# Streaming encoder step on one core: each half's first data loaded by the half ahead, semaphores cleared inside halves, another block order

## The reference: what is computed

```python
h = rms_norm(x, norm_g)
proj = h @ w_in        # 1024 -> 3912 columns, fifteen parts
# A: per query the 256 best keys by an indexer, softmax over these only
sc = relu(einsum('bthd,bsd->bths', iq, ik)); sc = einsum('bths,bth->bts', sc, iw)
sc = where(kpos // 64 <= qpos // 64, sc, -inf); idx = top_k(sc, 256)
ya = softmax(q . k[idx] / 8) @ v[idx] * silu(ag)      # 8 heads, 2 key heads
# B: gated linear recurrence (HGRN2), C: retention; each carries a 64x64 state per head
yb = rms_norm(gla(bq, 1 - f, bi, log f)) * silu(bg)
yc = rms_norm(retention(cq, ck, cv)) * silu(cg)
out = x + concat(ya, yb, yc) @ w_out
```

## Time and profile before

| | us |
|---|---|
| median of 3 runs (lowest, highest) | 3991.1 (3989.07, 3997.01) |
| the profiled execution's own time | 3998.49 |
| its span, first to last instruction | 3996.7 |
| TensorE busy | 3579.7 (90%) |
| VectorE busy | 2647.8 (66%) |
| ScalarE busy | 2324.3 (58%) |
| GpSimd busy | 1002.8 (25%) |
| mean granted clock of TensorE | 0.947 |

### The profile page before, as it was taken

One profiled execution on the slowest core, in us unless ns is written; L12 is line 12 of the kernel. 1 busy time (PEld: TensorE's weight loads), 2 busy tenths in 40 slices (PEclk: granted clock), 3 DMA queues, 4 the chain that ended last, 5 costly groups with the idle time before them and its releaser, 6 DMA issues. The chain is left out here.

```text
span 3996.7 us, 57114 instructions
## 1 busy us (share of the span) xinstructions
PE 3579.7 (90%) x17620; PEld 1677.0 (42%) x17620; DVE 2647.8 (66%) x6170; ACT 2324.3 (58%) x4386; POOL 1002.8 (25%) x1712
## 2 busy tenths in 40 slices
PE   6999999995789889898869999999768898899997
PEld 3555555551233333343335555555413333333433
DVE  7677777765766677565346666666666767776652
ACT  5333333335788888877323333333277888888762
POOL 0000000113543333334200000000145433333341
PEclk8999999996799999999989999999878999999998
DMA  5222222215201000011151111111152010000111
GB/s 187 86 79 80 79 80 79 78 55 137 79 24 35 31 24 21 22 38 36 39 201 37 38 39 39 42 38 34 36 131 78 18 39 23 23 25 20 39 39 39
DMA packets 175714, 226.60 MB, mean 57 GB/s; under 512 B 77632, under 2 KB 115520, under 8 KB 173696
## 3 DMA queue, kind: packets, MB, share of 16 engines
q1 hardware_dynamic: 175488, 224.06, 18.3%
HBM read 146.60 MB, written 77.38 MB: 56 GB/s over the span
## 5 line engine op out<-in xcount | busy, mean ns | idle before, releaser
L1524 ACT ACTIVATE signs<-sc,mid 128x1152 bf16<-128x1152 f32 (+14 forms) x720 | 974.9, 1355 | 278.4 <-POOL mid L1580 268.5
L426 PE MATMUL PJ<-w_in_hi,hTh 128*128 128x512 f16 (+2 forms) x2176 | 812.2, 373 | 18.4 <-DVE w_in_lo L937 16.7
L427 PE MATMUL PJ<-w_in_lo,hTh 128*128 128x512 f16 (+2 forms) x2176 | 810.8, 373 | 0.0
L429 PE MATMUL PJ<-w_in_hi,hTl 128*128 128x512 f16 (+3 forms) x1904 | 704.3, 370 | 0.0
L1429 PE MATMUL PV<-pt,va_p 128*65 128x512 f32 x1088 | 584.1, 625 | 73.3 <-ACT pt L1504 65.8
L1577 POOL TENSOR_SCALAR dlt<-cnta,stp 128x1 f32<-128x1 f32 (+1 forms) x720 | 293.0, 407 | 1075.9 <-ACT signs L1524 1072.5
L1672 DVE SCALAR_TENSOR_TENSOR sc<-rl,iwb,sc 128x512 f32<-128x512 f32 (+4 forms) x602 | 422.4, 718 | 208.3 <-ACT rl L1495 201.2
L1609 DVE CUSTOM_DVE_ANT_0 junkb<-AX,mneg 128x512 bf16<-128x512 f32 (+4 forms) x720 | 412.3, 601 | 74.1 <-PE AX L1374 55.0
L1580 POOL TENSOR_SCALAR mid<-mid,dlt,stp 128x1 f32<-128x1 f32 (+1 forms) x720 | 430.7, 598 | 75.6
L1495 ACT ACTIVATE rl<-AX 128x512 f32<-128x512 f32 (+5 forms) x688 | 347.1, 531 | 81.5 <-PE AX L1387 76.5
L1504 ACT ACTIVATE pt<-LG 128x512 f32<-128x512 f32 (+2 forms) x612 | 329.4, 553 | 92.8 <-PE LG L1414 88.4
(11 more groups left out here) (267 smaller groups left out, 5850.0 us busy)
## 6 DMA issues: line engine op xcount, KB each, us to landing
yt<-y_d SPq DMA_DIRECT2D x32, 512.0 KB, 3.5
out<-xr SPq DMA_DIRECT2D x32, 512.0 KB, 2.6
w_stage<-in SPq DMA_DIRECT2D x28, 512.0 KB, 4.1
w_d<-w_stage SPq DMA_DIRECT2D x56, 256.0 KB, 2.4
x<-in SPq DMA_DIRECT2D x16, 512.0 KB, 4.5
y_d<-ga SPq DMA_DIRECT2D x32, 256.0 KB, 2.0
q<-q_d SPq DMA_DIRECT2D x32, 256.0 KB, 2.9
stg<-in SPq DMA_DIRECT2D x32, 256.0 KB, 2.7
```

The costliest lines, as they stand in the source:

```text
L426: mm(out, hTh[:, par, c, 0:T], weights(g, c, wh), start=(c == 0), stop=False)
L427: mm(out, hTh[:, par, c, 0:T], weights(g, c, wl), start=False, stop=False)
L429: last = mm(out, hTl[:, par, c, 0:T], weights(g, c, wh), start=False, stop=(c == DC - 1))
L1524: A(signs[p][0:T, 0:W], sc[u % 3][0:T, 0:W], ACT.Sign, scale=-1.0, bias=small[u % 3]["mid"][0:T, :], accum_out=small[u % 3]["cnta"][0:T, : ...
```

## The change

*Buffers.* One tile `arena` as large as the 16 MB of weights, and x and the gains `ng`, now live through the whole kernel. The weights of a recurrent half fill the arena. In an attention half it holds the prompt's keys, queries, values, output weights, score buffers and others, laid out by hand (`in_arena`), so that the parts loaded first lie where the weights of groups that are used early lay. The row of ones is written once to device memory (`ones_d`) and loaded into the key tiles by DMA.

*Recurrence to attention.* While it is at block NB, SyncE loads for the attention half: the indexer's keys (4 DMAs), the first searched block's indexer queries and weights, the first q; behind the `kiT_c` wait the keys of both heads, the next indexer queries, two more q, the values. Only then do the stores of the keys of block NB follow. The states are stored a little earlier. The plan counts these loads as done.

*Attention to recurrence.* Ahead of the last store SyncE loads x of block 0, the gains and the weight groups 0 to 2 of the next layer (`next_layer`); the next half loads its constants and the groups 3 to 7.

*Semaphores.* Each half has its own set and GpSimd clears the other half's inside it; behind the last layer three engines share the rest.

*Order.* Another `seq`. *Retention.* Its transposes come behind the intra-chunk products, and `cqs` and `cqkT`'s copy accordingly.

The core of the diff:

```diff
+    BLOCKS = [1, 0, 3, 5, 7, 4, 6, 10, 12, 9, 11, 13, 14, 15, NB, 8, 2]
+    FIRST_SEARCHED = [b for b in BLOCKS if (b == NB and PAST + TS > K_S) or (b < NB and (b + 1) * P > K_P)][:2]
...
+    AHEAD = 3
...
+                if splits:
+                    load_x(0)
+                    sp.dma_start(ng[:], norm_g[l, :, :]).then_inc(gains, 16)
+                else:
+                    load_constants()
+                    for g in range(AHEAD, NG):
+                        load_group(go_own, g)
...
                     store_pairs(iq16_d, b, T, iqh, iql, st_iq)
+                    if b == NB:
+                        sp.wait_ge(proj, NG * NB + GI["cqk"] + 1)
+                        sp.wait_ge(st_ki, 64 * NB)
+                        load_prompt_keys(go_ahead, 2, 0)
+                        load_prompt_keys(go_ahead, 2, 1)
+                        sp.wait_ge(st_iq, 64 * NB)
+                        sp.wait_ge(st_v, 32 * NB)
+                        load_index_queries(go_ahead, 0, FIRST_SEARCHED[0])
+                        sp.wait_ge(proj, NG * NB + GI["iq"] + 1)
+                        sp.wait_ge(st_q, 64 * NB)
+                        load_queries(go_ahead, 0)
...
                     sp.wait_ge(kiT_c, b + 1)
+                    if b == NB:
+                        sp.wait_ge(proj, NG * NB + GI["kvi"] + 1)
+                        load_prompt_keys(go_ahead, 0, 0)
+                        load_prompt_keys(go_ahead, 1, 0)
+                        load_index_queries(go_ahead, 1, FIRST_SEARCHED[1])
+                        load_prompt_keys(go_ahead, 0, 1)
+                        load_prompt_keys(go_ahead, 1, 1)
+                        load_queries(go_ahead, 1)
+                        load_queries(go_ahead, 2)
+                        load_prompt_values(go_ahead, l)
+                        sp.wait_ge(sh_ok, 2 * NB + 1)
+                        for j in range(4):
+                            sp.dma_start(hg_s[l, j, :, :], head_square(S2, j)).then_inc(st_st, 16)
...
                     if b == 0 and prepares:
                         if splits:
                             sp.wait_ge(*low_done(len(chunks) - 1))
                         load_next(0)
+                    sp.wait_ge(yb_ok, 2 * b + 2)
...
                     project(t, T, par, "iq")
-                    pe.wait_ge(rpc_ok, t + 1)
-                    transposes(trv[1], [rpc[0:T, c * P:(c + 1) * P] for c in range(4)], T).then_inc(cqkT_ok, 1)
...
                     last.then_inc(atth_ok, 1)
+                    pe.wait_ge(rpc_ok, t + 1)
+                    transposes(trv[1], [rpc[0:T, c * P:(c + 1) * P] for c in range(4)], T).then_inc(cqkT_ok, 1)
                     project(t, T, par, "kvi")
...
                 rsqrt(x_ms, x_rs, rsx[:], ssx[:], 1)
+                for used in old:
+                    pool.sem_clear(used)
...
-            seq = [0, 1, 3, 8, 11, 9, 10, 12, 14, 13, 15, NB, 7, 6, 5, 4, 2]
+            seq = BLOCKS
...
+                    j0 = seq.index(0)
+                    sp.wait_ge(s["pair_ok"], len(items) - S_ITEM)
+                    sp.wait_ge(s["lo_ok"], S_ITEM)
+                    sp.wait_ge(s[f"b_st{j0 % 2}"], 16 * (j0 // 2 + 1))
+                    go_ahead(x_tile[:], xs[l + 1, 0:P, :], "x_in")
+                    go_ahead(ng_tile[:], norm_g[l + 1, :, :], "gains")
+                    sp.wait_ge(s["idx_ok"], before(NBLK, n_idx))
+                    sp.wait_ge(s["acc_ok"], before(NBLK, n_idx))
+                    for p in range(CHAINS):
+                        sp.wait_ge(s[f"cnt_ok{p}"], NIT * sum(chain(j) == p for j in searches))
+                    sp.wait_ge(s["mneg_ok"], max(j for j in searches if nth(j) % 3 < 2) + 1)
+                    for g in range(AHEAD):
+                        load_group(go_ahead, g)
+
                 for kind, j, k in order["SP"]:
+                    if (kind, j) == ("store", NBLK - 1) and l + 1 < DEPTH:
+                        next_layer()
...
-                pe.wait_ge(s["b_prep"], 1)
...
-                for c in range(2):
-                    for n in range(2):
-                        V.memset(keys[c][n][1][HD:HD + 1, :], 1.0)
...
-            with nc.Block() as block:
-                @block.gpsimd
-                def _(pool):
-                    for s in sems.values():
-                        pool.sem_clear(s)
+        left = list(sems["attention"].values())
+        with nc.Block() as block:
+            @block.gpsimd
+            def _(pool):
+                for used in left[0::3]:
+                    pool.sem_clear(used)
...
```

More of the change, by code:

```diff
@@ new lines, in load_prompt_keys @@
+    def load_prompt_keys(go, n, part):
+        a, b = KEY_PARTS[part]
+        for half in range(2):
+            dst, cols = prompt_keys(n, half), slice(a, b)
+            if n == 2:
+                go(dst[:, a:b], ik16_d[half, :, cols], f"kp{n}{part}")
+                continue
+            for r in range(2 - half):
+                go(dst[r * HD:(r + 1) * HD, a:b], k16_d[half, n * HD:(n + 1) * HD, cols], f"kp{n}{part}")
+        if n < 2 and part == 0:
+            go(prompt_keys(n, 1)[HD:HD + 1, :], ones_d[:, 0:SEQ], f"kp{n}{part}")
@@ new lines, in load_queries, with load_index_queries, load_prompt_values @@
+    def load_queries(go, j):
+        T = rows(BLOCKS[j])[1]
+        go(score_queries()[:, j % 3, 0:8 * T], q16_d[BLOCKS[j], :, 0:8 * T], f"b_q{j % 3}")
+    def load_index_queries(go, u, b):
+        T = rows(b)[1]
+        go(index_queries()[:, u % 2, 0:8 * T], iq16_d[b, :, 0:8 * T], f"b_iq{u % 2}")
+        go(index_weights()[0:T, u % 2, :], iw_d[b, 0:T, :], f"b_iq{u % 2}")
+    def load_prompt_values(go, l):
+        for h in range(2):
+            go(prompt_values()[:, :, h, 0:HD], v_p[l, :, h * HD:(h + 1) * HD].rearrange("(b p) d -> p b d", p=P), "b_vp")
@@ L1097, in paired @@
                 return (s["lo_ok"], i + 1) if i < S_ITEM else (s["pair_ok"], i - S_ITEM + 1)
+            LOADED = ([("load_key", n, part) for n in range(3) for part in range(2)] + [("load_q", j, 0) for j in range(3)]
+                      + [("load_idx", j, 0) for j in searches[:2]] + [("load_v", 0, 0)])
             def plan():
                 heads = {e: {} for e in ("SP", "PE", "ACT", "POOL", "DVE")}
+                seen = {}
                 def job(eng, kind, j, k, cost, wish, *needs, line=""):
+                    if (kind, j, k) in LOADED:
+                        seen[kind, j, k] = 0.0
+                        return
                     heads[eng].setdefault(f"{kind}{line}", []).append(((kind, j, k), cost, wish, needs))
@@ L1203, in plan @@
                 lag = {"SP": 5000, "PE": 250, "ACT": 180, "POOL": 200, "DVE": 120}
-                seen, clock, order, banks = {}, dict.fromkeys(heads, 0.0), {e: [] for e in heads}, []
+                clock, order, banks = dict.fromkeys(heads, 0.0), {e: [] for e in heads}, []
                 at = {(e, kind): 0 for e in heads for kind in heads[e]}
@@ L1316, in key_columns @@
                         go(dst[0:HD], k16_d[half, n * HD:(n + 1) * HD, cols], name)
-                def load_key(n, part):
-                    a, b = KEY_PARTS[part]
-                    for half in range(2):
-                        key_columns(keys[0][n][half][:, a:b], n, half, slice(a, b), f"kp{n}{part}")
                 def load_new_keys(_, __):
@@ L1748, in _ @@
                 sp.wait_ge(lb_in, 32)
+                sp.wait_ge(lb_ones, 1)
+                sp.dma_start(ones_d[:, :], row[:]).then_inc(lb_ones, 16)
+                sp.wait_ge(lb_ones, 17)
             @block.scalar
@@ L1774, in _, with half_sem, one @@
                 step(nc.vector.tensor_scalar(oml[:], lbt[:], -1.0, 1.0, ALU.mult, ALU.add))
-        sems = {}
-        def layer_sem(name):
-            if name not in sems:
-                sems[name] = sem(name)
-            return sems[name]
-        for l in range(DEPTH):
-            recurrent_half(l, layer_sem)
-            attention_half(l, layer_sem)
-            with nc.Block() as block:
-                @block.gpsimd
-                def _(pool):
-                    for s in sems.values():
-                        pool.sem_clear(s)
+        sems = {"recurrent": {}, "attention": {}}
+        def half_sem(half):
+            def one(name):
+                if name not in sems[half]:
+                    sems[half][name] = sem(name)
+                return sems[half][name]
+            return one
+        of_recurrent, of_attention = half_sem("recurrent"), half_sem("attention")
+        for l in range(DEPTH):
+            recurrent_half(l, of_recurrent, of_attention, list(sems["attention"].values()))
+            attention_half(l, of_attention, of_recurrent, list(sems["recurrent"].values()))
+        left = list(sems["attention"].values())
[3 more added lines that the diff above has]
+                for used in left[0::3]:
+                    pool.sem_clear(used)
+            @block.vector
+            def _(dve):
+                for used in left[1::3]:
```

(5 more changed lines are left out.)

152 lines of the change are left out of this document (89 added, 63 removed).

## The result

The changed kernel takes 3980.6 us in the median of 7 runs, the kernel before 3995.1 (one of its 7 runs took 9142.6 us and is left out of the ratio): a ratio of 0.9969, 95% interval 0.9957 to 0.9981. By the ratio that is 12 us, where I forecast 44. The direction and the range held; the size didn't.

A forecast was written before the change was run, and what follows sets the result against it. TensorE, by far the busiest engine, bounds the kernel; time can come only from its idle stretches, slow clock and joints. Terms -9.5 - 20.5 + 12 - 6 - 20 = -44 us, from the 3991.1 median to 3947; range 3895 to 3990.

The forecast's parts named there:

- Semaphores at the end: Behind the last layer: three engines clear 20 each, about 1.9 us with the barrier against 11.4, so -9.5 us.
- Attention 0 to recurrence 1: Joint and following half: earlier start, no wait for gains and x, less waiting on weights and late x; -20.5 us.
- rival E: End of attention 0: the last store waits behind 6 MB of loads, up to 10 us later, 3957 us; chance 0.12.
- Recurrence to attention: Joint in each layer: moved loads stand ahead of the last stores in SyncE's queue; +6 us each, +12 in all.
- D: Recurrence to attention: issuing costs next to nothing when data engines are free; -8.8 instead of +6 per layer, 3917 us; chance 0.08.
- Retention: Recurrence 0: transposes moved behind the intra-chunk products cover all but the longest of TensorE's waits for `cks`; -6 us.
- Order: Attention halves: new block order removes part of the 49 us of waiting at block 3; -10 each, -20 us.
- Rival C: Attention halves: searches bound small blocks 5, 7, 4 and 6, 92 us too much per half; 4023 us, chance 0.12.
- B: Attention halves: starvation goes entirely, small blocks keep the pace; -39 instead of -10 each, 3889 us; chance 0.18.

The follow-up runs named there:

- experiment 2: The kernel before with only retention's transposes, ScalarE's copy and VectorE's product moved behind the intra-chunk products: ratio 0.9965 to the kernel before.
- experiment 6: The kernel after without attention 0's loads ahead for recurrence 1 (x, gains, three weight groups loaded at that half's start): ratio 0.9991 to the kernel before.
- experiment 3: The kernel after with 20 of the 27 loads for the attention half issued by ScalarE's queue behind its last copy: ratio 0.9908 to the kernel before.
- experiment 5: The kernel after with the planner counting loads as before and 20 loads on ScalarE's queue: 0.9843; then 18 loads in SyncE's wait, 9 on ScalarE's: 0.9811.
- before's plan: The kernel after, new order, planner counting the attention half's loads as the kernel before did, dropping them from SyncE's list afterwards: 3955.6 us, ratio 0.9895.
- experiment 1: The order alone: the kernel before with only the new order of blocks, ratio 0.9963; the kernel after with the old order, 0.9918, both to the kernel before.

## Why the prediction was off

*Semaphores at the end*: -9.5 forecast, -9.5 measured. In the halves they hid: the first diagonal product comes 9.4 us behind the indexer's first matmul, before 9.9.

*Attention 0 to recurrence 1*: -20.5 forecast. Measured -16.1 in the joint and -6.2 in recurrence 1 (its 7.5 less 1.3 for the retention; experiment 2 alone gives 2.1 for this part, experiment 6 leaves 1.0): -22.3. The last store wasn't held up (rival E), since the cover was 17 us. Block 1's x still took long to land, 21.1 instead of 25.0 us, but was asked for early enough.

*Recurrence to attention*: +6 each (5.5 by the sum), measured +7.1 each, within the bounds of 1 and 12. The sum had 16.4 us for the 27 loads and they took 16.7; the 1.6 us over 5.5 are about what the state's first store took more behind the values (2.41 us for 0.60). By D, in which issuing costs next to nothing, the indexer would have started 8.8 us earlier; the trace and experiments 3 and 5 show the opposite. The Trainium skill, "DMA: Bandwidth & Descriptors", section "Issuing engines are not separate DMA queues", says that the time to initiate a DMA is usually small relative to the DMA. The trace disagrees here: a state's store takes 0.60 us to issue and has landed 1.8 us from its start, and 27 issues in a row add up to the 16.7. The same section of the Trainium skill says that DMAs started from several engines at once save only the sequencers' time, on the same DMA engines. That agrees: this saved 10.7 us of each joint (29.7 to 19.0), net of the 4 us by which the last store landed later.

*Retention*: -6, measured -12.3. The waits were sized rightly (6.1 of 6.3 went). What I left out is that behind a 3.2 us stop TensorE ran at a lower clock for a while: 3.4 us in the 12 behind it.

*Order*: the step that failed: "so I take -10 for each half, -20 us", where +9.6 and +2.4 were measured. With before's plan the new order gains 7 us a half (1075 against 1082, means of 8 and 6 halves). That this is near 10 is luck. I had capped the gain of 49 us at the start by TensorE's idle time and left the rest as it was; in attention 1 of experiment 1 the first three blocks gave 37, the blocks 5, 7, 4 and 6 took 68 back, and the eight large ones gave 45. What the step lacked most is the planner. I read the change's `seen[kind, j, k] = 0.0` as bookkeeping, and priced it at nothing without saying so. It gives every engine another list for 1,080 us, which cost 15 us a half. The kernel with before's plan ran at 3955.6 us (its kernel before: 3997.7), -42 where the forecast was -44. This too is partly luck: retention gave 6 us more than forecast, and the order and the joints recurrence to attention gave 4 us less each.

*Rival C* was right on its mechanism (71 of 92 us in the four blocks) and wrong on its price: I counted the searches that now bound the small blocks, not that the large ones behind would then run at 6.0 us a key block instead of 6.45. B's full repair didn't come: 38 of the 49 us at the start did, but the small blocks didn't keep the pace.

## What to carry to other kernels

When a greedy planner writes the instruction lists, any edit to its inputs is a change to the whole stage: price it as unknown by 1 to 2% either way, compare lists before believing a local argument, and try several starting shifts, since the best of them (2.1% faster than the kernel before, with the joints repaired) came from a shift that stands for nothing in the kernel. Work moved ahead of a barrier is free only in a queue's idle time: the same 27 loads made a joint 7 us longer than before when they stood in SyncE's queue ahead of the last stores, and 9 us shorter when spread over SyncE's waits and ScalarE's queue. And count the clock with a stop of TensorE: here one of 3.2 us cost 6.6.

## What the runs showed of the hardware

A stop of 3.2 us was followed by 12 us at a mean clock of 0.72, in the kernel before and again in it with the new order, while the six shorter waits for `cks` in recurrence 0 (3.1 us together, the longest 1.4) left it at 1.00 between 200 and 800 us. ScalarE's queue issues most DMAs in the same 0.4 to 0.6 us as SyncE's, both at once: between 2845.1 and 2857.6 of experiment 3 ScalarE issued 18 loads and began on the values, SyncE its last 20 stores. The transfers do slow each other: SyncE's last store took 6.2 us to land there, 1.9 in the kernel after. Semaphores are cleared one every 71 ns by GpSimd, 66 by ScalarE and 83 by VectorE (the last block of the kernel after), so the clears that I couldn't price cost about as much as GpSimd's. Executions of the same list, in three kernels, differ by up to 7 us in a half (1085.7 to 1093.0 for that of the kernel after), so a single trace can't tell two lists 5 us apart.
